# A weight ring of 22 slots plus two used once, in the place where the experts' sums are kept later

## What is computed

```python
def expert_choice_ffn(h, w_router, w_gate, w_up, w_down):      # h: rms_norm(x) * gain
    cap = EC_CAPACITY * S // N_EXPERTS                          # 64 tokens for each of 16 experts
    aff = softmax(h @ w_router)                                 # [tokens, experts]
    g, idx = top_k(aff.T, cap)
    xe = h[idx]                                                 # gather: 64 rows per expert
    hid = silu(xe @ w_gate) * (xe @ w_up)                       # 1024 -> 2048
    ye = (hid @ w_down) * g
    return zeros_like(h).at[idx].add(ye)                        # scatter-add
x = x + expert_choice_ffn(rms_norm(x, g_ffn), ...); out = rms_norm(x, g_final)
```

## Time and profile before

| what | us |
|---|---|
| median of 3 runs (lowest, highest) | 2025.66 (2024.54, 2026.27) |
| the profiled execution | 2027.24 |
| its span, first to last instruction | 2025.4 |
| TensorE busy | 1891.7 (93%) |
| VectorE, ScalarE, GpSimd busy | 715.2, 519.0, 67.4 |
| bytes moved | 504.86 MB, 61.5% of what 16 DMA engines could carry in the span |

### The profile page before, as it was taken

One profiled execution on the slowest core, in us unless ns is written; L12 is line 12 of the kernel. 1 busy time (PEld: TensorE's weight loads), 2 busy tenths in 40 slices (PEclk: granted clock), 3 DMA queues, 4 the chain that ended last, 5 costly groups with the idle time before them and its releaser, 6 DMA issues.

```text
span 2025.4 us, 20605 instructions
## 1 busy us (share of the span) xinstructions
PE 1891.7 (93%) x8728; PEld 1142.1 (56%) x8728; DVE 715.2 (35%) x1121; ACT 519.0 (26%) x810; POOL 67.4 (3%) x58
## 2 busy tenths in 40 slices
PE   7999999999999999999996999988889988888998
PEld 6788888888886788866873333333223333222332
DVE  6544544333456765776444111101111110111111
ACT  5444322222344443376522000000000000000001
POOL 2000000000013001000110000000000000000000
PEclk9999999999999999999998999999999999999999
DMA  5221322322323142112355999999999999999997
GB/s 184 84 83 63 125 94 94 103 95 94 110 75 110 63 163 78 63 53 88 142 240 206 427 427 427 427 428 426 429 427 426 429 426 427 428 427 427 427 427 296
DMA packets 59259, 504.86 MB, mean 249 GB/s; under 512 B 7520, under 2 KB 8416, under 8 KB 31520
## 3 DMA queue, kind: packets, MB, share of 16 engines
q1 hardware_dynamic: 58592, 503.01, 61.5%
q10 hardware_dynamic: 576, 0.53, 0.1%
HBM read 499.32 MB, written 4.19 MB: 249 GB/s over the span
## 4 chain that ended last, share of the span: by engine, by line
PE 61%; DMA 25%; issue 7%; DVE 3%; ACT 3%; POOL 1%; ACTq 0%; DVEq 0%; POOLq 0%
PE ps L1967 32%; DMA ring_a<-in_experts_in 18%; PE ps L2305 8%; PE ps L2316 8%; DMA ring_b<-in_experts_in 6%; PE ps L1910 4%; PE ps L2266 3%; PE ps L2288 1%; PE ps L2325 1%; POOL xacc L723 1%; DVE d_lo L1190 1%; POOL gbl L757 0%; ACT hidT L1158 0%; ACT d_hi L779 0%; PE ps L2087 0%
## 5 line engine op out<-in xcount | busy, mean ns | idle before, releaser
L2305 PE MATMUL ps<-ring_a,xe 128*64 128x512 f32 x1408 | 316.4, 596 | 44.7 <-DMA ring_a<-in_experts_in 43.9
L1190 DVE TENSOR_TENSOR d_lo<-d_raw,d_hi 128x1024 fp32r<-128x1024 f32 x166 | 208.1, 1263 | 122.9 <-ACT d_hi L779 122.3
L2305 PEld LDWEIGHTS ps<-ring_a,xe 128*64 128x64 f32 x1408 | 97.1, 137 | 259.3 <-issue 191.5
L1410 DVE TENSOR_TENSOR hid<-hid,ps 128x512 f32<-128x512 f32 x32 | 20.6, 684 | 455.8 <-PE ps L2305 455.8
L1967 PE MATMUL ps<-n_hi,d_hi 128*128 128x512 f32 x448 | 176.0, 393 | 1.5 <-DVE d_lo L1190 0.8
L1967 PE MATMUL ps<-n_hi,d_lo 128*128 128x512 f32 x448 | 174.4, 389 | 0.0
L1967 PE MATMUL ps<-n_lo,d_hi 128*128 128x512 f32 x448 | 174.3, 389 | 0.0
L779 ACT ACTIVATE d_hi<-d_raw 128x1024 fp32r<-128x1024 f32 x166 | 170.9, 1050 | 7.3 <-DMA d_raw<-in_tiles_in 6.8
L2305 PE MATMUL ps<-ring_b,xe 128*64 128x512 f32 x640 | 147.7, 607 | 25.5 <-DMA ring_b<-in_experts_in 25.5
L2316 PE MATMUL ps<-ring_a,hidT 128*64 128x512 f32 x704 | 157.6, 595 | 6.4 <-ACT hidT L1158 3.9
L1831 DVE TENSOR_TENSOR x<-x,ps 128x1024 f32<-128x1024 f32 x60 | 69.2, 1216 | 264.3 <-PE ps L2288 264.3
(11 more groups left out here) (457 smaller groups left out, 2658.0 us busy)
## 6 DMA issues: line engine op xcount, KB each, us to landing
ring_a<-in_experts_in SPq DMA_DIRECT2D x114, 2048.0 KB, 41.1
ring_b<-in_experts_in SPq DMA_DIRECT2D x57, 2048.0 KB, 41.0
d_raw<-in_tiles_in SPq DMA_DIRECT2D x166, 512.0 KB, 3.3
ring_a<-in_experts_in SPq DMA_DIRECT2D x36, 1024.0 KB, 35.6
ring_b<-in_experts_in SPq DMA_DIRECT2D x6, 1024.0 KB, 11.4
x_in<-in_xT_in SPq DMA_DIRECT2D x4, 512.0 KB, 7.0
x<-in_xT_in SPq DMA_DIRECT2D x1, 2048.0 KB, 9.5
x_store<-x SPq DMA_DIRECT2D x1, 2048.0 KB, 8.8
```

Source lines behind the costliest of these rows:

```text
L1190: dve.tensor_tensor(d_lo[:, n % SLOTS, :, :], d_raw[:, n % SLOTS, :, :], d_hi[:, n % SLOTS, :, :].bitcast(F32), ALU.subtract).then_inc(t_l ...
L1410: return dve.tensor_tensor(out, a, b, ALU.mult)
L2305: mm = pe.matmul(ps[half * CAP:(half + 1) * CAP, 2 * m + q, :], xe[:, k, :], slot(e, n)[:, (2 * q + half) * S:(2 * q + half + 1) * S], sta ...
```

## The change

The ring gets 22 slots (14 in `ring_a` with two late ones, 6 in `ring_b`), and chunks 22 and 23 go into `acc`, a tensor of 16 KB that later holds the experts' sums. So 24 chunks can be loaded before the first is used; afterwards the ring has 22 places, and `acc` takes no further weights. The 16 KB for it come from `h2`, which is gone: the gather reads `x2` itself, and the rms factor is multiplied into a second choice matrix `picks`, four `tensor_scalar` instructions of 128x64 ahead of the `pick` in every `choose`. `x2` is only read from then on; the first expert's sums are x2 + product, written to `acc`, later ones acc + product. The 24 KB for the three slots come from 16 KB of the strip at address 0 (now 128 bytes) and from the place of `hid`, `hidT` and the mask tensors, which move among the small tiles. Slots 12 and 13 are new among those loaded before the end of `out2`, slot 20 and 21 are the late ones. There are 207 moves, 26 single ones at the start.

```diff
-RING, RING_A, RING_B = 19, 12, 6
+RING, RING_A, RING_B = 22, 14, 6
+LATE = RING - RING_A - RING_B
+EXTRA = 2
+SCRATCH = 128
+def place_of(g):
+    return g if g < RING else RING if g < RING + EXTRA else (g - EXTRA) % RING
+def freed(g):
+    v = g - EXTRA - RING
+    return (v if v < RING else v + EXTRA) + 1
 def ring_moves():
-        n = 1 if g < RING + 2 or g >= end - 4 or g % RING in (RING_A - 1, RING - 2) else 2
+        n = 1 if g < RING + EXTRA + 2 or g >= end - 4 or place_of(g) in (RING_A - 1, RING_A + RING_B - 1) else 2
...
+            kb += 16 if kb >= 192 else 0
-        ring_a = at("ring_a", [P, RING_A + 1, FF], 88)
+        ring_a = at("ring_a", [P, RING_A + LATE, FF], 80)
-        h2 = at("h2", [P, TT, D], 48)
+        acc = at("acc", [P, TT, D], 48)
-        hid = at("hid", [P, 2, S], 80)
-        hidT = at("hidT", [P, 2, 4, P], 84)
+        hid = at("hid", [P, 2, S], 201.5)
+        hidT = at("hidT", [P, 2, 4, P], 201.5)
+        picks = at("picks", [P, TT, CAP], 205.5)
...
         def slots(g, n):
-            s = g % RING
-            if RING_A <= s < RING - 1:
+            s = place_of(g)
+            if s == RING:
+                return acc[:, 2 * (g - RING):2 * (g - RING) + 2, :].rearrange("p s f -> p (s f)")
+            if RING_A <= s < RING - LATE:
...
                     g, n = MOVES[m]
-                    if g + n > RING:
-                        sp.wait_ge(s_used, g + n - RING)
+                    if g >= RING + EXTRA:
+                        sp.wait_ge(s_used, freed(g + n - 1))
...
             load_weights(5, RING_A)
             stage_done(sp, "out2", 7)
-            load_weights(RING_A, RING - 1)
+            load_weights(RING_A, RING - LATE)
             sp.wait_ge(t_pe.sem, t_pe.count("x3"))
-            load_weights(RING - 1, len(MOVES))
+            load_weights(RING - LATE, len(MOVES))
...
-            for t in range(TT):
-                act.wait_ge(t_act.sem, t_act.count(f"x{t}"))
-                t_act.done(act.activation(h2[:, t, :], x2[:, t, :], ACT.Copy, scale=esm[:, 8 + t:9 + t]), f"h{t}")
...
             def choose(e):
+                for t in range(TT):
+                    x_dve.done(dve.tensor_scalar(picks[:, t, :], iot[:, :], pos[:, t, e:e + 1], esm[:, 8 + t:9 + t],
+                                                 ALU.is_equal, ALU.mult), f"picks{t}")
                 x_dve.done(dve.tensor_tensor(pick[:, :, :], at, number, ALU.is_equal), "pick")
...
             def placed(e):
-                    row = x2[:, t, :].rearrange("p (d c) -> p d c", d=2)
-                    e_dve.done(dve.tensor_tensor(row, row, ps[:, b:b + 2, :], ALU.add), f"o{t}")
+                    row, old = (a[:, t, :].rearrange("p (d c) -> p d c", d=2) for a in (acc, acc if e else x2))
+                    e_dve.done(dve.tensor_tensor(row, old, ps[:, b:b + 2, :], ALU.add), f"o{t}")
...
             def gather(e):
-                pe.wait_ge(x_dve.sem, x_dve.count("pick", e))
+                pe.wait_ge(x_dve.sem, x_dve.count(f"picks{TT - 1}", e))
-                        mm = pe.matmul(ps[d * CAP:(d + 1) * CAP, 5, :], pick[:, t, :], h2[:, t, d * S:(d + 1) * S],
+                        mm = pe.matmul(ps[d * CAP:(d + 1) * CAP, 5, :], picks[:, t, :], x2[:, t, d * S:(d + 1) * S],
...
-    nc = bacc.Bacc("TRN2", target_bir_lowering=False, num_devices=1)
+    nc = bacc.Bacc("TRN2", target_bir_lowering=False, num_devices=1, dynamic_dma_scratch_size=SCRATCH)
```

More of the change, by code:

```diff
@@ L307, in kernel_program @@
         x1 = at("x1", [P, KD, S], 176)
-        R = at("R", [P, S], 204.75)
+        R = at("R", [P, S], 204.6875)
         junk = at("junk", [P, GH, GDV], 124)
@@ L392, in kernel_program @@
         iot = at("iot", [P, CAP], 207.25)
-        top8 = at("top8", [NE, 8], 207.5)
+        top8 = at("top8", [NE, 8], 193.875)
         aw = at("aw", [NE, S], 202.5)
-        awm = at("awm", [NE, S], 80)
-        awc = at("awc", [NE, S], 82)
+        awm = at("awm", [NE, S], 194.5)
+        awc = at("awc", [NE, S], 196.5)
         xe = at("xe", [P, KD, CAP], 194.5)
-        xg = at("xg", [P, S], 196.5)
-        pick = at("pick", [P, TT, CAP], 198.5)
-        pickg = at("pickg", [P, TT, 2, CAP], 199.5)
-        hid = at("hid", [P, 2, S], 80)
-        hidT = at("hidT", [P, 2, 4, P], 84)
[L403 to L407, removed]
+        xg = at("xg", [P, S], 199.5)
+        pick = at("pick", [P, TT, CAP], 196.5)
+        picks = at("picks", [P, TT, CAP], 205.5)
+        pickg = at("pickg", [P, TT, 2, CAP], 197.5)
+        hid = at("hid", [P, 2, S], 201.5)
+        hidT = at("hidT", [P, 2, 4, P], 201.5)
+        ye = at("ye", [P, S], 199.5)
+        place = at("place", [P, S], 197.5)
+        zsq = at("zsq", [P, D], 4)
+        gbc = at("gbc", [P, D], 0)
+        fin = at("fin", [P, TT, D], 16)
         ident = at("ident", [P, P], 192)
@@ L415, in kernel_program @@
         dsm = at("dsm", [P, 64], 194.25)
-        m01 = at("m01", [P, 2, P], 206.75)
+        m01 = at("m01", [P, 2, P], 206.6875)
         scr = [at(f"scr{n}", [P, S + 4], 194.5 + 2.03125 * n) for n in range(5)]
@@ L554, in kernel_program @@
         t_pe = Steps(sem("route_pe"), ["rf", "partA", "part", "logits", "x0", "x1", "x2", "affT", "x3", "posT"])
-        t_act = Steps(sem("route_act"), [f"sq{k}" for k in range(KD)] + ["root", "exp"] + [f"x{t}" for t in range(TT)]
-                      + [f"h{t}" for t in range(TT)])
+        t_act = Steps(sem("route_act"), [f"sq{k}" for k in range(KD)] + ["root", "exp"] + [f"x{t}" for t in range(TT)])
         t_dve = Steps(sem("route_dve"), ["dgf", "rf", "rwg", "part", "raw", "mx", "sub", "rstd", "lg", "sum", "rec", "aff"]
@@ L560, in kernel_program @@
         t_pool = Steps(sem("route_pool"), ["zero", "zero1", "one", "sel1", "sel2", "sel3", "iota"])
-        s_ring = [sem(f"ring_in{s}") for s in range(RING)]
+        s_ring = [sem(f"ring_in{s}") for s in range(RING + EXTRA)]
         s_used = sem("ring_used")
@@ L564, in kernel_program @@
         x_act = Steps(sem("gather_act"), ["xg"], 16)
-        x_dve = Steps(sem("gather_dve"), ["pick", "xe"], 16)
+        x_dve = Steps(sem("gather_dve"), [f"picks{t}" for t in range(TT)] + ["pick", "xe"], 16)
         e_pe = Steps(sem("expert_pe"), ["hT", "place", "o0", "o1", "o2", "o3"], 15)
@@ L595, in slots @@
         def slots(g, n):
-            s = g % RING
-            if RING_A <= s < RING - 1:
+            s = place_of(g)
+            if s == RING:
+                return acc[:, 2 * (g - RING):2 * (g - RING) + 2, :].rearrange("p s f -> p (s f)")
+            if RING_A <= s < RING - LATE:
                 rows = ring_b[:, s - RING_A:s - RING_A + n, :]
             else:
-                s = (s + 1) % RING
+                s = (s + LATE) % RING
                 rows = ring_a[:, s:s + n, :]
@@ L612, in last_row @@
         def last_row(t):
-            return x2[:, t, :].rearrange("p (d c) -> p d c", d=2) if t == 1 else last_pair(t)
+            return acc[:, t, :].rearrange("p (d c) -> p d c", d=2) if t == 1 else last_pair(t)
         def tiles4(ap):
@@ L652, in load_weights @@
                     g, n = MOVES[m]
-                    if g + n > RING:
-                        sp.wait_ge(s_used, g + n - RING)
+                    if g >= RING + EXTRA:
+                        sp.wait_ge(s_used, freed(g + n - 1))
                     src = experts_in[g * P * FF:(g + n) * P * FF].rearrange("(p f) -> p f", p=P)
-                    sp.dma_start(slots(g, n), src).then_inc(s_ring[m % RING], 16)
+                    sp.dma_start(slots(g, n), src).then_inc(s_ring[m % (RING + EXTRA)], 16)
             load1(0)
@@ L2257, in _ @@
             t_pe.done(mm, "posT")
-            pe.wait_ge(t_act.sem, t_act.count(f"h{TT - 1}"))
+            pe.wait_ge(t_act.sem, t_act.count(f"x{TT - 1}"))
             def gather(e):
-                pe.wait_ge(x_dve.sem, x_dve.count("pick", e))
+                pe.wait_ge(x_dve.sem, x_dve.count(f"picks{TT - 1}", e))
                 if e >= 2:
@@ L2277, in chunk @@
                 m = MOVE_OF[e * PER + n]
-                pe.wait_ge(s_ring[m % RING], (m // RING + 1) * 16)
+                pe.wait_ge(s_ring[m % (RING + EXTRA)], (m // (RING + EXTRA) + 1) * 16)
             def place_turned(e):
@@ L2328, in residual @@
             def residual(t, d, bank):
-                pe.matmul(ps[:, bank, :], ident[:, :], x2[:, t, d * S:(d + 1) * S], start=True, stop=False, skip_group_check=True)
+                pe.matmul(ps[:, bank, :], ident[:, :], acc[:, t, d * S:(d + 1) * S], start=True, stop=False, skip_group_check=True)
             gather(0)
```

## The result

| | before | after |
|---|---|---|
| median, us (lowest to highest, runs) | 2025.97 (2024.54 to 2026.63, 4) | 2007.32 (2006.39 to 2010.19, 4) |
| ratio of the runs, 95% interval | | 0.9913 (0.9901 to 0.9925) |
| profiled execution, its span | 2027.24, 2025.4 | 2007.87, 2006.1 |

The kernel became faster by 18.65 us.

A forecast was written before the change was run, and what follows sets the result against it. The weight stream at DMA's ceiling, plus a fixed tail, was taken to set the end. 2027.24 - 12.25 (five chunks) + 0.6 (`picks`) = 2015.6 for the profiled execution, so a median of 2014.0 us, range 2012.0 to 2018.9.

The forecast's parts named there:

- the stream's pace: Weights passing after the restart, when the first chunk is used: 2.45 us per chunk, as in the kernel before.
- The lead: Ahead of the restart: five more chunks loaded, each taking 2.45 us off the end, a gain of 12.25 us.
- All 24 chunks in before the restart: Two gaps without bytes ahead of the experts: added chunks end at 1059 and 1095.2, 9 us before the restart.
- The dry stream: Rival at the second expert: the ring runs empty, only three places count, 2018.9 us; cover 2.1 us, chance 0.08.
- The choice matrices: Four `picks` instructions before the first gather: 1.0 us in place of 0.43, restart 0.6 us later; hidden in other experts.
- Scaled rows, sums, the tail: ScalarE's four activations gone (4.28 us, off the path), first expert's sum and the end reading `acc`: no gain or cost.
- The strip: Rival: the shrunken strip at address 0 adds 1.8 us to each of 181 moves, +326 us, 2340; chance 0.03.
- What would show it: Signs in the profile: queue issues, filled windows, TensorE's first wait after 1360, DMA waits some 60 us, pairs at 4.9 us.

The follow-up runs named there:

- e9_after288: The changed kernel with all tiles 32 bytes higher (base 288), so that no slot begins at a multiple of 256 bytes; 2013.40 us, ratio 0.9943.
- e1_low: The kernel before with the strip cut to 128 bytes, so that every tile lies 16,256 bytes lower; 2018.50 us, ratio 0.9968.
- e3_base16384: The kernel before with the strip cut to 128 bytes and tiles from 16,384 bytes on, 128 lower; 2019.38 us, ratio 0.9969.
- e12_before_aligned: The kernel before with its full strip, start of tiles rounded up to a multiple of 256 bytes, two small tiles moved 64 bytes; 2018.94 us, ratio 0.9969.
- e2_strip: The kernel before with the strip cut to 128 bytes but the tiles left at their old addresses; 2025.09 us, ratio 0.9998.
- e7_base16448: The kernel before with the small strip and tiles from 16,448 bytes on, so slots begin 64 bytes beyond a multiple of 8,192; 2024.55 us, ratio 1.0000.
- e5_after: The changed kernel run once more with nothing altered, as the measure for runs beside it; 2006.74 us, ratio 0.9905 to the kernel before.
- e6_extra0: The changed kernel without the two places used once (EXTRA 0), a ring of 22 and a lead of 22 chunks; 2012.23 us, ratio 0.9931.
- e11_split: The changed kernel with 15 unused matmuls in the search, one before the first gather, and the gather waiting for each quarter of picks separately; 2003.78 us, ratio 0.9892.
- e10_warm2: The changed kernel with 15 unused matmuls in the search and two more before the first gather; 2005.57 us, ratio 0.9903.
- e8_warm: The changed kernel with 12 unused matmuls on TensorE while VectorE searches for the best tokens; 2006.67 us, ratio 0.9906.
- e4_lead19: The changed kernel with move 19 and all behind it waiting for the first chunk to be used, so the lead is 19 again; 2017.76 us, ratio 0.9963.

## Why the prediction was wrong

**The step that failed** is the stream's pace in the sum. It says "From that moment 365 MB have to pass at 2.45 us each", and the sum then charges the 346 chunks behind the restart with the price of the kernel before, so that it has a term for the chunks that are missing and none for those that are left. I looked at the shrunken strip as a danger to the queue only, and not at what it does to the addresses: the start of the tiles went from 16,512 to 256 bytes, from 128 bytes beyond a multiple of 256 to none. 346 chunks at 6.9 us in all (857.5 - 850.6), 0.020 each, are the missing term: 2014.0 - 6.9 = 2007.1, measured 2007.32; so close a fit is partly luck, since each term is known to some half a microsecond only. e9_after288 takes exactly this out of the change, and e1_low, e3_base16384 and e12_before_aligned put it into the kernel before.

A rule for it was at hand. The Trainium skill ("DMA: Bandwidth & Descriptors", How a descriptor splits into AXI transactions) says that descriptors are cut at multiples of 256 bytes, so that one that starts elsewhere needs one more. It speaks of reads; here the edits leave the sources in HBM alone, and the place that moved is the one written. The runs agree with it in kind: in the traces the packets of 16,384 bytes take 617.1 ns on average before, 617.0 in e2_strip, 617.1 at 64 bytes beyond and 617.8 at 32, but 613.2 after, 613.2 in e1_low and 613.5 in e12_before_aligned. By the Trainium skill's count of beats the cost would depend on the offset (as an estimate, 4 beats on 512 for 128 bytes, 0.8%, and 1 beat, 0.2%, for 32); measured are 0.6% at 64 and at 128 and 0.75% at 32, so the wasted bytes do not set it. That the address sets the pace is shown by the runs; that the extra piece is the reason is not.

Point by point, the rest of the prediction:

- *The lead, 12.25 us.* Right to about half a microsecond. Under the old pace the change brings 2025.49 - 2013.40 = 12.1 us net of `picks`, where the sum had 11.65 (e9_after288). From the restart to the last wait, the traces at the old pace take 869.3 and 869.1 us with 19 chunks loaded (e2_strip, e7_base16448) and 857.5 with 24, 2.34 per chunk; at the new pace 862.5 with 19 (e1_low) and 850.6 and 850.2 with 24 (changed kernel, e5_after), 2.4 per chunk. The profiled execution of the kernel before took 870.8, as its DMA came up more slowly (403 GB/s in the first 52 us, 411 and 410 in e2_strip and e7_base16448). So the 19.3 us between the two profiled executions hold some 1 us that belongs to neither lead nor addresses.
- *All 24 chunks in before the restart.* Right: the first gap is filled until about 1059, the second until about 1095. But of the windows I foretold "some 6 MB" and "some 5" where the sum's own end times (1095.2 and 1059) give about 2.6 and 1.7, and 2.8 and 1.9 were measured: a slip, without effect on the time.
- *The dry stream.* It did not come. The move after the extra places is issued at 1157.72, and DMA stays at 418 and 442 GB/s in the windows around it; e6_extra0 shows the places' full worth.
- *The choice matrices, 1.0 us for four.* Measured 0.98, a step of 0.22. TensorE's idle time before the gather went from 0.94 to 1.50: 0.56 us. The restart itself came 0.88 later (1103.89, 1104.77), 0.26 of it already there at the moves after x3 (1078.08, 1078.34).
- *Scaled rows, sums, the tail.* No trace of a cost: the last wait to the end is 50.8 us in both.
- *The strip.* Cutting it to 128 bytes slows no transfer of this kernel: 0.9998. (The rival counts 181 moves after the restart; it is 207 - 24 = 183, as two of the 26 single moves go behind it. That changes nothing.)
- *What would show it.* "The forecast is wrong if the pairs come at another pace than 4.9 us": they did, and this was the right place to look. TensorE first waits at 1406.93 (foretold: after 1360), and its waits for DMA sum to 56.2 (foretold 60).

## What to carry to other kernels

Where a stream at its ceiling sets the end, every chunk loaded ahead of its start is worth a chunk's time, and so, as far as seen, is every us by which it starts sooner (3.6 us gave 3.7 at the last wait in e11_split, but 2.6 gave only 1.4 in e10_warm2); look for DMA's empty windows ahead of it and for memory that is free only until then. When tiles change place, work out their first byte modulo 256: here the builder's first free byte, rounded up to 32, put 400 MB of transfers on slow addresses, and rounding it up to 256 was worth some 6 us by itself (e12_before_aligned: 5.5 between the medians, 6.3 by the ratio). And if a sum has a term for what is removed, ask what could change the price of what remains.

## What the runs showed of the hardware that was not expected

- Packets of 16 KB into SBUF take 0.6 to 0.75% more time (617.0 to 617.8 ns instead of 613.1 to 613.5) when they start 32, 64 or 128 bytes beyond a multiple of 256 bytes, nearly alike for all three. The source is the same in all runs, so nothing is shown of its address.
- TensorE's granted clock fell to 0.5 of full speed (1.2 of 2.4 GHz) although it had been busy 11.0 of 14 us before, after gaps of 3.3 and 1.5 us with 0.4 us of work between (e8_warm). With gaps of 0.7 us it stayed at 1.00 from 1089 to 1099 (e11_split).
- In the profiled execution of the changed kernel one longer wait for a pair, behind waits of 1.1 to 1.3 us, was followed by the low clock: granted were 0.57 on average from 1912 to 1916, and the pair took 5.35 us instead of 3.65. The stream did not lose by it: from the restart to the last wait it took 850.6 us, and 850.2 in e5_after, where this did not happen.

```profile
1911.62 5.35 PE L2322 MATMUL ps<-ring_b,xe 128*64 128x512 f32 x16 [2.35 <-DMA ring_b<-in_experts_in]
```

- The clock fell late in some executions too: in the profiled one of e10_warm2 the last expert's `down` took 15.65 us instead of 13.95, with these windows at its start:

```profile
1976.00:1980.00 4.00, 3.17 (x9) 1.14 (x10) 0.69 (x1) 0.60 (x1) 0.00 (x0) 0.63 0.99 420
1980.00:1984.00 4.00, 4.00 (x20) 1.69 (x18) 0.00 (x0) 0.00 (x0) 0.00 (x0) 0.95 0.70 294
```

  It follows the two waits of 0.8 us around the transposes of `hid`, which the executions without it have as well. The same 15.65 us stand in the profiled executions of e6_extra0 and e8_warm, and 13.95 in those of the changed kernel, e4_lead19, e5_after, e9_after288 and e11_split. It costs 1.7 us when it comes, and a part of the spread of runs may be this; that is not shown.
